# The end of the state-space mixer: another order of ScalarE's work, of the weight preparation and of the first GLU products

## The reference, cut to what matters

```python
bu = einsum('blgp,gnp->blgn', u, b_bar)             # 64 groups of 16 features, 64 complex states each
states = scan(x_t = lam_bar * x_{t-1} + bu_t)
y = real(einsum('blgn,gpn->blgp', states, c_mat)) + d_skip * u
g = gelu(y)
mix = (g @ w_glu_a) * sigmoid(g @ w_glu_b)          # 1024 x 1024 each
```

## Time and profile before

| what | value |
|---|---|
| three executions | 1206.24, 1208.85, 1210.62 us; median 1208.85 |
| profiled execution, its own time | 1210.54 us |
| its span, first to last instruction | 1208.4 us |
| mean granted TensorE clock | 0.986 of full |
| TensorE matmul busy | 1144.9 us (95%) |
| VectorE, ScalarE, GpSimd busy | 551.6, 410.5, 185.8 us |

### The profile page before, as it was taken

One profiled execution on the slowest core, in us unless ns is written; L12 is line 12 of the kernel. 1 busy time (PEld: TensorE's weight loads), 2 busy tenths in 40 slices (PEclk: granted clock), 3 DMA queues, 4 the chain that ended last, 5 costly groups with the idle time before them and its releaser, 6 DMA issues.

```text
span 1208.4 us, 20385 instructions
## 1 busy us (share of the span) xinstructions
PE 1144.9 (95%) x8339; PEld 1029.3 (85%) x8339; DVE 551.6 (46%) x821; ACT 410.5 (34%) x698; POOL 185.8 (15%) x137
## 2 busy tenths in 40 slices
PE   4399889999999999999999989989999999999997
PEld 4388789999999999999999867668888888888886
DVE  5677624554333343334444355455443443434443
ACT  5723222333222222223333355543323232323332
POOL 3979300002111111100000000000211112110000
PEclk9999879999999999999999999999999999999999
DMA  7225422232322323222233311113323332223322
GB/s 134 74 63 104 103 81 95 73 103 71 104 82 92 104 69 104 66 80 80 95 95 105 123 36 36 37 36 105 101 75 102 104 104 85 88 74 96 96 96 90
DMA packets 119385, 104.61 MB, mean 87 GB/s; under 512 B 21868, under 2 KB 117216, under 8 KB 119008
## 3 DMA queue, kind: packets, MB, share of 16 engines
q1 hardware_dynamic: 109544, 99.72, 27.0%
q10 hardware_dynamic: 9792, 4.19, 1.5%
HBM read 98.11 MB, written 5.24 MB: 86 GB/s over the span
## 4 chain that ended last, share of the span: by engine, by line
issue 44%; PE 43%; DVE 4%; DMA 4%; POOL 2%; ACTq 2%; ACT 2%; SPq 0%; POOLq 0%; DVEq 0%
PE banks L1288 40%; DMA y_feat<-y_dram 2%; ACTq L693 2%; POOL gate L566 2%; DMA y_dram<-y_act 1%; DMA raw_c_re<-in_ssm_c_re 1%; PE banks L1408 1%; ACT u_row L623 1%; PE banks L1403 1%; PE banks L1350 0%; PE banks L1351 0%; ACT y_act L677 0%; PE banks L1313 0%; DVE pow_t L974 0%; ACT w_high L588 0%
## 5 line engine op out<-in xcount | busy, mean ns | idle before, releaser
L588 ACT CAST w_high<-raw 128x1024 fp32r<-128x1024 f32 x188 | 197.1, 1049 | 583.3 <-PE banks L1288 583.2
L889 DVE TENSOR_TENSOR w_low<-raw,w_high 128x1024 fp32r<-128x1024 f32 x188 | 230.8, 1228 | 216.8 <-ACT w_high L588 216.8
L1288 PE MATMUL banks<-x_high,w_high 128*128 128x512 f32 (+2 forms) x1184 | 320.8, 324 | 1.0 <-DVE x_low L1103 1.0
L1288 PE MATMUL banks<-x_high,w_low 128*128 128x512 f32 (+2 forms) x1184 | 318.3, 322 | 0.0
L1288 PE MATMUL banks<-x_low,w_high 128*128 128x512 f32 (+2 forms) x1184 | 317.4, 321 | 0.0
L1288 PEld LDWEIGHTS banks<-x_high,w_high 128*128 128x128 f32 x1184 | 198.9, 189 | 19.3 <-issue 2.2
L1288 PEld LDWEIGHTS banks<-x_low,w_high 128*128 128x128 f32 x1184 | 198.7, 188 | 16.1
L1288 PEld LDWEIGHTS banks<-x_high,w_low 128*128 128x128 f32 x1184 | 198.1, 188 | 16.7
L1288 PE MATMUL banks<-a_high,w_high 128*128 128x256 f32 (+2 forms) x528 | 140.4, 320 | 0.0
L1288 PE MATMUL banks<-a_high,w_low 128*128 128x256 f32 (+2 forms) x528 | 140.2, 320 | 0.0
L1288 PE MATMUL banks<-a_low,w_high 128*128 128x256 f32 (+2 forms) x528 | 140.2, 320 | 0.0
(11 more groups left out here) (270 smaller groups left out, 1232.5 us busy)
## 6 DMA issues: line engine op xcount, KB each, us to landing
raw<-in_ffn_w_gate SPq DMA_DIRECT2D x22, 1024.0 KB, 5.2
raw<-in_ffn_w_up SPq DMA_DIRECT2D x22, 1024.0 KB, 5.1
raw<-in_ffn_w_down SPq DMA_DIRECT2D x16, 768.0 KB, 4.5
raw<-in_ffn_w_down SPq DMA_DIRECT2D x16, 640.0 KB, 4.4
raw<-in_attn_w_qkv SPq DMA_DIRECT2D x6, 1024.0 KB, 5.0
raw<-in_ssm_w_glu_b SPq DMA_DIRECT2D x4, 1024.0 KB, 5.7
raw<-in_ssm_w_glu_a SPq DMA_DIRECT2D x4, 1024.0 KB, 5.4
k_toep<-k_dram SPq DMA_DIRECT2D x64, 64.0 KB, 2.9
```

Of the source, the lines that this page charges most:

```text
L588: nc.scalar.copy(w_high[:, j], raw[:, slot, :, j * P:(j + 1) * P]).then_inc(w_rounded, 1)
L889: nc.vector.tensor_tensor(w_low[:, j], raw[:, slot, :, j * P:(j + 1) * P], w_high[:, j], ALU.subtract).then_inc(w_split, 1)
L1288: ins = nc.tensor.matmul(banks[:, bank + h, b0:b0 + cn], w[:, j, k, :], xx[:, first_k + k, c0 + base:c0 + base + cn], start=start and k == ...
```

## The change

On ScalarE, the GELU and the store of batch b-1 open iteration b, followed by the start column and the copy of the lags of batch b+1, and the rounding of y is put one batch later (round_input(b-2) ahead of load_outputs(b-1)). The copy of the last lags and the casting of weight block 0 stand at the end of iteration 5, that of block 1 in iteration 6. After the loop come gelu, store, round_input of the batch before and load_outputs for batches 6 and 7, and the last round_input. On VectorE, block 0 is split at the end of iteration 5, and block 1 in iteration 6 behind the state of batch 6, after a wait for the last lag products. On TensorE, the lags of batch 7 go ahead of the second half of batch 5's outputs, and four of the six early units of block 0 are put between the halves of the outputs of batches 6 and 7: k 0 and 1, then k 2, then k 3. SP issues four of the eight loads of y_feat of batch 6 too, with semaphores of their own. d_diag moves to the memory of `w_low[:, 1]`.

```diff
--- before.py
+++ after.py
@@ -119,6 +119,7 @@
         powers.close()
         w_high = sb("w_high", [P, 2, KB, P], F32R, align=STREAM_LINE)
         skip = ExitStack()
+        sb("w_low_first", [P, KB, P], scope=skip, align=STREAM_LINE)
         d_diag = sb("d_diag", [2 * GROUP, PAIRS, GROUP], scope=skip)
         skip.close()
         w_low = sb("w_low", [P, 2, KB, P], F32R, align=STREAM_LINE)
@@ -281,6 +282,7 @@
         turn_ready, read_ready = sem("turn_ready"), sem("read_ready")
         v_ready, k_ready, k_copied, zeros_made = sem("v_ready"), sem("k_ready"), sem("k_copied"), sem("zeros_made")
         d_ready, state_ready, y_ready, gelu_ready, y_placed, y_stored, bbar_placed = sem("d_ready"), sem("state_ready"), sem("y_ready"), sem("gelu_ready"), sem("y_placed"), sem("y_stored"), sem("bbar_placed")
+        y_halves = [sem("y_half0"), sem("y_half1")]
         gt_rounded, gt_split, pairs_cleared = sem("gt_rounded"), sem("gt_split"), sem("pairs_cleared")
         fine_ready, powers_ready, k_stored, zeros_stored = sem("fine_ready"), sem("powers_ready"), sem("k_stored"), sem("zeros_stored")
 
@@ -418,12 +420,12 @@
                         if b + 1 < BATCHES:
                             place_lags(b + 1)
                 if i == 1:
-                    b = BATCHES - 1
-                    sp.wait_ge(y_stored, 16 * BATCHES)
-                    sp.wait_ge(gt_split, b - 1)
-                    for g in range(GB // 2, GB):
-                        sp.dma_start(y_feat[g * GROUP:(g + 1) * GROUP, b % 2],
-                                     y_dram[b, :, :, g, :].rearrange("s q c -> q s c")).then_inc(y_placed, 16)
+                    for b in range(BATCHES - 2, BATCHES):
+                        sp.wait_ge(y_stored, 16 * (b + 1))
+                        sp.wait_ge(gt_split, b - 1)
+                        for g in range(GB // 2, GB):
+                            sp.dma_start(y_feat[g * GROUP:(g + 1) * GROUP, b % 2],
+                                         y_dram[b, :, :, g, :].rearrange("s q c -> q s c")).then_inc(y_halves[b % 2], 16)
                 load_tile(i, 0, by_rows(w_glu_b[0])[:, :, 2 * P * i:2 * P * (i + 1)], wait=i > 0)
                 load_tile(i, 1, by_rows(w_glu_a[0])[:, :, 2 * P * i:2 * P * (i + 1)], wait=i > 0)
 
@@ -689,13 +691,15 @@
                 act.wait_ge(y_stored, 16 * (b + 1))
                 if b >= 2:
                     act.wait_ge(gt_split, b - 1)
-                for g in range(GB if b < BATCHES - 1 else GB // 2):
+                for g in range(GB if b < BATCHES - 2 else GB // 2):
                     nc.scalar.dma_start(y_feat[g * GROUP:(g + 1) * GROUP, b % 2],
                                         y_dram[b, :, :, g, :].rearrange("s q c -> q s c")).then_inc(y_placed, 16)
 
             def round_input(b):
 
-                act.wait_ge(y_placed, 16 * GB * (b + 1))
+                act.wait_ge(y_placed, 16 * (GB * (b + 1) - GB // 2 * max(0, b + 3 - BATCHES)))
+                if b >= BATCHES - 2:
+                    act.wait_ge(y_halves[b % 2], 16 * GB // 2)
                 nc.scalar.copy(glu_high[:, b], y_feat[:, b % 2].rearrange("p s c -> p (s c)")).then_inc(gt_rounded, 1)
 
             read_starts(0)
@@ -705,24 +709,30 @@
             side(0)
             front(1)
             side(1)
-            for b in range(BATCHES):
+            for b in range(BATCHES - 1):
+                if b >= 1:
+                    gelu(b - 1)
+                    store_outputs(b - 1)
                 if b + 2 < BATCHES:
                     read_starts(b + 2)
-                if b + 1 < BATCHES:
                     lags(b + 1)
+                else:
+                    round_weights(QUAD_GLU, 1, wait=False)
+                if b >= 2:
+                    round_input(b - 2)
                 if b >= 1:
                     load_outputs(b - 1)
                 if b + 2 < BATCHES:
                     side(b + 2)
                     front(b + 2)
-                if b >= 1:
-                    round_input(b - 1)
-                if b == BATCHES - 2:
+                if b + 2 == BATCHES - 1:
+                    lags(BATCHES - 1)
                     round_weights(QUAD_GLU, 0, wait=False)
-                    round_weights(QUAD_GLU, 1, wait=False)
+            for b in range(BATCHES - 2, BATCHES):
                 gelu(b)
                 store_outputs(b)
-            load_outputs(BATCHES - 1)
+                round_input(b - 1)
+                load_outputs(b)
             round_input(BATCHES - 1)
             def updated(k, m, n, gain):
 
@@ -1082,12 +1092,14 @@
 
                 if b + 2 < BATCHES:
                     make_injection(b + 2)
+                if b == BATCHES - 2:
+                    dve.wait_ge(k_ready, BATCHES)
+                    split_weights(QUAD_GLU, 1)
                 if 2 <= b < BATCHES - 1:
                     split_input(b - 2)
-            dve.wait_ge(k_ready, BATCHES)
-            split_weights(QUAD_GLU, 0)
+                if b == BATCHES - 3:
+                    split_weights(QUAD_GLU, 0)
             split_input(BATCHES - 3)
-            split_weights(QUAD_GLU, 1)
             split_input(BATCHES - 2)
             split_input(BATCHES - 1)
             dve.wait_ge(read_ready, BATCHES)
@@ -1411,10 +1423,10 @@
                 if PB - 1 in pairs:
                     ins.then_inc(y_ready, 1)
 
-            def early_glu(off):
-
-                product(QUAD_GLU, off, 0, GLU_EARLY, glu_high, glu_low, 2 * off, L, stop=False, used=False,
-                        each=lambda k: pe.wait_ge(gt_split, k + 1))
+            def early_glu(off, k0, k1):
+
+                product(QUAD_GLU, off, 0, k1 - k0, glu_high, glu_low, 2 * off, L, start=k0 == 0, stop=False, used=False,
+                        w_k=k0, each=lambda k: pe.wait_ge(gt_split, k + 1))
 
             for b in range(2):
                 for h in range(2):
@@ -1432,11 +1444,17 @@
                 outputs(b, (0, 1))
                 if b + 2 < BATCHES:
                     injection(b + 2, 1)
-                outputs(b, (2, 3))
                 if b + 2 == BATCHES - 1:
                     lags(BATCHES - 1)
-            early_glu(0)
-            early_glu(1)
+                if b == BATCHES - 2:
+                    early_glu(0, 0, 2)
+                if b == BATCHES - 1:
+                    early_glu(0, 3, 4)
+                outputs(b, (2, 3))
+                if b == BATCHES - 2:
+                    early_glu(0, 2, 3)
+            early_glu(0, 4, GLU_EARLY)
+            early_glu(1, 0, GLU_EARLY)
             for k in range(GLU_EARLY, KB):
                 pe.wait_ge(gt_split, k + 1)
                 for off in range(2):
```

## The result

The changed kernel takes 1215.93 us (median of 20 runs, 1206.79 to 1218.46), the kernel before 1210.12 us (median of 20, 1206.24 to 1214.55). The ratio is 1.0036, with a 95% interval of 1.0019 to 1.0053: **slower by 0.36%**. The forecast was 1213, with 1203.5 to 1216.5 as range. The runs of the changed kernel are of two groups, a shape that the median doesn't tell: four of 20 take 1206.8 to 1207.6 us (mean granted clock 0.992), fourteen 1215.5 to 1218.5 (0.978 to 0.983), two lie between. Seven of the 20 are above the range's 1216.5.

A forecast was written before the change was run, and what follows sets the result against it. TensorE was taken to lose time to idleness and the half clock at the mixer's end. State at 143.9, last outputs 168.0, products 179.3 against 175.3: 4 us slower, 1212.8 from the 1208.85 median, said as 1213; range 1203.5 to 1216.5.

The forecast's parts named there:

- Part 3: VectorE's split of block 0, ahead of batch 6's state, waits for its casting: a new TensorE wait of 6.0 us.
- The chain: Read table 134.7, lag products 0.9, lag copy 0.35, casting 1.05, splitting 1.25, state 5.6: batch 6's state ends at 143.9.
- The sum behind the chain: At half clock, additions 2.0, four output halves 16.8, four units 5.3: last outputs end at 168.0; twelve units left, 179.3.
- All that follows is unchanged: After block 0's products, the castings and splittings of the next blocks and everything later stay as before.
- The first rival: The full clock comes back between the last outputs: 6 us faster, 1204.5 by the profile, 1202.8 by the median; chance 0.19.
- The rule weighed: The skill's rule that keeping TensorE busy brings the full clock, here among the last outputs; price as in the first rival.
- Parts 1, 2 and 5: ScalarE's order: GELU waits of 6.16 and 0.91 us can go; earlier last lag products: slack only; SP's loads: nothing by itself.
- part 4: Four early units of block 0 between the last outputs: same work, only earlier, taken at half clock, 1.32 us each.

The follow-up runs named there:

- split_behind_state: The changed kernel with VectorE's split of weight block 0 moved behind the state of batch 6: 1204.69 us, ratio to the kernel before 0.9947.
- cast_earlier: The changed kernel with ScalarE's casting of block 0 put ahead of the loads of batch 4, some 8 us earlier: 1211.92 us, ratio 0.9985.
- lags_behind: The changed kernel with the last lag products again behind the second half of batch 5's outputs: 1215.82 us, ratio to the kernel before 1.0049.
- splits_behind_all: The changed kernel with block 0's split behind batch 6's state, batch 4's glu_low and block 1's split behind batch 7's: 1201.19 us, ratio 0.9915.
- filler_in_stall: The changed kernel with six useless dense matmuls in TensorE's wait before the additions of batch 7: 1207.41 us, ratio to the kernel before 0.9971.
- early_units_behind: The changed kernel with all six early units of block 0 behind the last outputs: 1214.50 us, ratio to the kernel before 1.0036.
- part 1 alone: The kernel before with only ScalarE's new order of GELU, store, rounding and castings: 1207.33 us, ratio to the kernel before 0.9966.
- undoing part 2: The run lags_behind, the changed kernel with the last lag products put back behind batch 5's outputs: 1215.82 us, ratio 1.0049.
- filler alone: The kernel before with five idle matmuls ahead of the outputs of batch 7: 1208.91 us, ratio to the kernel before 0.9987.
- the version with the least waiting: The kernel splits_behind_all with the last lag products behind the second half of batch 5's outputs: 1200.77 us, ratio to the kernel before 0.992.

## Why the prediction was right

The time is in the range, and the sign is the likeliest one, with the mechanism that was named. But it lies 0.6 us under the range's upper end, and 14 of 20 runs happened to be of the kind forecast; had most been of the other kind, the median would have been 1207, still within a range 13 us wide, but faster than the kernel before. By its own steps:

- **Part 3, the step that decides,** is confirmed twice. The profile shows the wait for w_high ahead of the state (6.55 us, said: about 8; glu_low of batch 4 took 2.27 us instead of 0.7 and ate the difference) and TensorE's wait for the state (5.82, said: 6.0). And split_behind_state moves that split alone, and TensorE's wait is gone.
- **The chain** was forecast to end at 143.9 and ended at 144.8. The 0.9 us are in its first term: GpSimd's last table was ready at 135.7, not 134.7. Its tables for batch 7 started at 125.67, when those of batch 6 were just done, where I had let them start at the end of state 5 (124.6). Already the batch before was late, by states that wait for the later roundings (0.29 us of TensorE's wait at 115.74), and the glu_low ahead of state 4 took 2.05 us (at 108.04), not the 0.7 of the sum. The rest, 144.8 less 135.7, is 9.1 us, against 9.15 in the sum.
- **The sum behind the chain:** said 24.1 us from the additions to the end of the last outputs, measured 24.04 (144.90 to 168.94). The additions at half clock, which no row of before had, took 1.96 us (said 2.0). Two terms missed and cancelled: the four halves of outputs took 16.3 us (said 16.8), the four units among them 5.8 (said 5.3). The twelve units left took 11.1 us to the start of the wait for w_low (182.32 less 2.25, less 168.94), said 11.3. At the end the forecast was 4.0 us slower, and block 2 starts 4.6 us later.
- **"All that follows is unchanged"** was not quite right: the clock fell again at 184 behind the wait of 2.25 us for w_low, where it hadn't in the trace of before. By the stretches of 2 us from 182 to 188 (0.96, 0.50 and 0.68) that is 1.7 us of full clock lost. Between the two profiled executions there are 5.35 us (1215.89 less 1210.54): 4.6 at the start of block 2, the 1.7, and about 1 us less elsewhere. The kernel before has a stretch of half clock that the changed one lacks (0.53 from 798 to 800, 0.61 from 800 to 802), which is of that size. The second fall isn't in every execution of kernels of this kind: the profiles of cast_earlier, lags_behind and splits_behind_all have it, those of split_behind_state, filler_in_stall and early_units_behind don't.
- **The first rival,** that the clock comes back between the outputs, had a chance of 0.19 and a price of 10 us against the forecast. The four low runs of 20, at the time of filler_in_stall, are 9 us below the rest; lags_behind's profile shows that the clock can come back there. It seems to be no alternative to the forecast, as I had put it, but what the same kernel does in a part of its runs. That the four runs themselves were such is argued, as none of them was profiled: their granted clock of 0.992 is above the 0.989 of lags_behind's profile and close to the 0.993 of filler_in_stall, so the clock came back sooner in them than there, or fell later.
- **The rule weighed:** the row of 154 to 156 again has TensorE busy 2.00 of 2.00 at 0.50, so being busy wasn't enough, as argued. Its price, 6 us faster than the kernel before, wasn't reached either: the four low runs are 3 us and filler_in_stall is 4 us faster than the kernel before. The prediction puts 6 us of busy outputs at half clock against the rule; by the earlier trace rows it is 8.4 (152.64 to 161.01).
- **Parts 1, 2 and 5** cost nothing by themselves, as said: part 1 alone gains 0.34%, and undoing part 2 makes no gain. Part 5 was not run alone. For part 4, early_units_behind has the same ratio as the changed kernel.

The point was 2.9 us low (1213 against 1215.9). 1.3 of it are the base: the median of the three runs shown was 1208.85, that of 20 is 1210.12. The rest is the chain's 0.6 and a part of the second fall.

## What to carry to other kernels

When an instruction is put earlier on an engine that works in order, ask what it waits for, not how long it takes: a split of 1.2 us, waiting for its casting, held the state behind it by more than 7, and with it behind that state 11 us came back. A wait of TensorE must be priced with the clock that goes with it and with the work that follows it: ahead of small matmuls with a weight load each, 5.8 us of waiting cost 10 us more. In single profiles the clock also fell behind waits of 1.3 to 2.2 us, but that these waits did it isn't shown. And the clock can only be cashed in where the next chain allows it: filler alone gave the kernel before 0.13%, not told from nothing, ScalarE's order alone 0.34%, and the version with the least waiting 0.8%.

## What the runs showed of the hardware that I had not expected

- VectorE's instructions with two inputs from SBUF and GpSimd's took turns. In the changed kernel glu_low<-y_feat,glu_high began at 129.20, 0.2 us behind a GpSimd instruction of 1.93 us, and took 2.27 us, ending 0.6 us behind it (0.70 at 145.80, with GpSimd idle). In the kernel before one began at 118.03, 0.02 us ahead of GpSimd's read_t: it took 0.71 and read_t 2.48, where it takes 1.92 at 108.51. Another of the kernel before, at 128.78, took 1.34 and ended 0.6 us behind GpSimd's read (127.63 and 1.94 us), with ScalarE issuing no loads then (they begin at 131.37), so the loads aren't the cause. The w_low of 2.94 us in cast_earlier fits as well. No run was made for this alone.
- The same program, on the same chip, has groups of runs 9 us apart (1207 and 1216) which by their granted clocks (0.992, and 0.978 to 0.983) differ in how long it was at half, and single runs up to 18 us apart in cast_earlier. A median of three runs can fall on either side.
- The clock was at half for as long behind a wait of 2.2 us (cast_earlier, 137.8 to 171.9) as with one of 5.8 us (changed kernel, 139.5 to 173.6): 34.1 us in both. TensorE worked through nearly all of it in cast_earlier and was idle for 5.4 us of it in the changed kernel, so the half clock cost more in the first, and the start of block 2 came out the same (182.33 and 182.32).
